# Start addresses of matmul operand tiles moved apart by 32 to 256 bytes, and two weight units multiplied in token halves

## What is computed

```python
# first block
p = rms_norm(x, norm1_g) @ w_in                  # then attention, gated delta, two gated linear mixers
x = x + mixed @ w_out
x = x + conv_glu_ffn(rms_norm(x, norm2_g), w_up, ffn_conv_w, ffn_conv_b, w_down)
# second block
h = h + short_conv_mixer(rms_norm_2(h, g), conv_w_in, conv_w, conv_w_out)
h = h + swiglu_ffn(rms_norm_2(h, g), conv_ffn_w13, conv_ffn_w2)
h = h + mla_mixer(rms_norm_2(h, g), w_dq, ..., w_o, k_nope, k_pe, v, cos, sin)
h = h + swiglu_ffn(rms_norm_2(h, g), mla_ffn_w13, mla_ffn_w2)
return rms_norm_2(h, final_norm_g)
```

## Time and profile before

| what | value |
|---|---|
| time, median of 2 runs | 1940.74 us (1940.49 to 1941.0) |
| span of the profiled execution | 1938.3 us |
| TensorE busy | 1890.5 us, 98% of the span |
| TensorE weight loads busy | 1540.8 us, 79% |
| VectorE, ScalarE, GpSimd busy | 959.2, 739.5, 237.1 us |
| TensorE in the chain that ended last | 91% |
| mean granted TensorE clock | 0.986 of full |
| bytes moved by DMA | 161.34 MB, mean 83 GB/s |

### The profile page before, as it was taken

One profiled execution on the slowest core, in us unless ns is written; L12 is line 12 of the kernel. 1 busy time (PEld: TensorE's weight loads), 2 busy tenths in 40 slices (PEclk: granted clock), 3 DMA queues, 4 the chain that ended last, 5 costly groups with the idle time before them and its releaser, 6 DMA issues.

```text
span 1938.3 us, 25963 instructions
## 1 busy us (share of the span) xinstructions
PE 1890.5 (98%) x9271; PEld 1540.8 (79%) x9271; DVE 959.2 (49%) x1354; ACT 739.5 (38%) x1075; POOL 237.1 (12%) x196
## 2 busy tenths in 40 slices
PE   8989999999999999999999999999999999999998
PEld 6778867667888888888888888888776778888887
DVE  6464466654777763344454444333647444444322
ACT  6542543554444443232253333232455343333222
POOL 0051000102111111000021111101000121111100
PEclk9999998999999999999999999999999999999999
DMA  6310211113333333333333333333320133333332
GB/s 193 87 33 1 55 34 34 34 47 89 103 97 97 94 94 94 98 98 98 98 88 104 94 95 97 92 99 101 92 83 22 44 95 94 94 96 96 100 90 73
DMA packets 309223, 161.34 MB, mean 83 GB/s; under 512 B 12688, under 2 KB 306832, under 8 KB 309024
## 3 DMA queue, kind: packets, MB, share of 16 engines
q1 hardware_dynamic: 308080, 157.67, 28.1%
q0 software_dynamic: 640, 2.17, 0.3%
q10 hardware_dynamic: 432, 0.52, 0.1%
HBM read 158.24 MB, written 2.10 MB: 83 GB/s over the span
## 4 chain that ended last, share of the span: by engine, by line
PE 91%; DVE 4%; ACT 3%; issue 1%; POOL 0%; DMA 0%; ACTq 0%; DVEq 0%; POOLq 0%
PE ps L371 26%; PE ps L372 26%; PE ps L373 26%; PE ps L1063 1%; PE ps L1743 1%; PE ps L1491 1%; PE ps L1075 1%; PE ps L1501 1%; PE ps L2039 1%; PE ps L2040 1%; PE ps L1734 1%; PE ps L936 1%; ACT whi L358 1%; PE ps L920 1%; PE ps L1455 0%
## 5 line engine op out<-in xcount | busy, mean ns | idle before, releaser
L371 PE MATMUL ps<-xhi,whi 128*128 128x512 f32 x1656 | 656.6, 396 | 3.1 <-ACT ecol L989 2.1
L372 PE MATMUL ps<-xlo,whi 128*128 128x512 f32 x1656 | 647.7, 391 | 0.0
L373 PE MATMUL ps<-xhi,wlo 128*128 128x512 f32 x1656 | 647.6, 391 | 0.0
L358 ACT ACTIVATE whi<-raw 128x1024 fp32r<-128x1024 f32 (+2 forms) x297 | 309.0, 1040 | 707.6 <-PE ps L373 707.0
L366 DVE TENSOR_TENSOR wlo<-raw,whi 128x1024 fp32r<-128x1024 f32 (+2 forms) x297 | 365.8, 1232 | 278.6 <-ACT whi L358 278.6
L371 PEld LDWEIGHTS ps<-xhi,whi 128*128 128x128 f32 x1656 | 313.1, 189 | 72.1 <-issue 7.9
L373 PEld LDWEIGHTS ps<-xhi,wlo 128*128 128x128 f32 x1656 | 312.8, 189 | 65.9
L372 PEld LDWEIGHTS ps<-xlo,whi 128*128 128x128 f32 x1656 | 313.1, 189 | 65.3 <-issue 2.2
L621 DVE TENSOR_TENSOR zS<-ps,rs 128x512 f32<-128x512 f32 x132 | 91.3, 692 | 296.8 <-PE ps L373 284.6
L373 PE MATMUL ps<-h_hi,wlo 128*128 128x512 f32 x528 | 205.4, 389 | 0.0
L371 PE MATMUL ps<-h_hi,whi 128*128 128x512 f32 x528 | 205.4, 389 | 0.0
(11 more groups left out here) (339 smaller groups left out, 1718.7 us busy)
## 6 DMA issues: line engine op xcount, KB each, us to landing
raw<-in_conv_ffn_w SPq DMA_DIRECT2D x52, 512.0 KB, 3.8
raw<-in_mla_ffn_w SPq DMA_DIRECT2D x52, 512.0 KB, 3.8
raw<-in_w_up SPq DMA_DIRECT2D x44, 512.0 KB, 3.8
raw<-in_w_in SPq DMA_DIRECT2D x28, 512.0 KB, 3.8
raw<-in_conv_w_in SPq DMA_DIRECT2D x24, 512.0 KB, 3.7
raw<-in_w_down SPq DMA_DIRECT2D x16, 448.0 KB, 3.5
raw<-in_conv_ffn_w SPq DMA_DIRECT2D x16, 448.0 KB, 3.5
raw<-in_mla_ffn_w SPq DMA_DIRECT2D x16, 448.0 KB, 3.4
```

Source lines behind the costliest of these rows:

```text
L358: a.activation(whi[:, u % PARTS, 0:n], raw[:, u % RAW, 0:n], ACT.Copy).then_inc(hi_split, 1)
L371: t_.matmul(out, wh, xh, start=first, stop=False)
L372: t_.matmul(out, wh, xl, start=False, stop=False)
L373: return t_.matmul(out, wl, xh, start=False, stop=last)
```

## The change

Three things are done.

1. Empty tiles (`gap_...`) are put between tiles, and `raw`, `whi` and `wlo` are cut into one tensor per place, so that `whi0`/`wlo0` (even units) and `whi1`/`wlo1` (odd units) start at different addresses modulo 512. Indexing changes from `whi[:, u % PARTS, ...]` to `whi[u % PARTS][:, ...]`. No instruction is added by it.
2. In units 9 and 10 of `w_in` each matmul over 512 tokens becomes two over 256: first all 8 slices of tokens 0 to 255, then all 8 of tokens 256 to 511. The weights of a slice are loaded once for each half. The waits and the semaphore at the end are the same.
3. All tiles behind move with the gaps.

The start of each operand tile modulo 512 bytes, from the sizes in the order of the calls:

| tile | before | after |
|---|---|---|
| `xT`, `xhi` | 128 | 128 |
| `xlo` | 128 | 192 |
| `raw`, `whi` and `wlo` of even units | 128 | 192 |
| `whi` and `wlo` of odd units | 128 | 448 |
| `h_hi` | 128 | 0 |
| `h_lo` | 128 | 64 |
| `c_hi` | 128 | 0 |
| `c_lo` | 128 | 32 |
| `h3_hi` | 128 | 32 |
| `h3_lo` | 128 | 96 |
| `mx`, `kn`, `qn`, `qp`, `vtok`, `lhi`, `chi` | 128 | 0 |
| `cst` (`hsum`, `ones` start 516 and 1028 bytes behind it) | 128 | 448 |
| `sq`, `ssq`, `rs`, `xg` | 160 | 480 |

The distance of a streamed slice from the weight slice that is used with it (streamed start less weight start, modulo 512) was 0 for all products of `passes`. Now it is, for even and odd units: `xhi` 448 and 192, `xlo` 0 and 256, `h_hi` 320 and 64, `h_lo` 384 and 128, `c_hi` 320 and 64, `c_lo` 352 and 96, `h3_hi` 352 and 96, `h3_lo` 416 and 160.

```diff
--- before.py
+++ after.py
@@ -247,10 +247,13 @@
 
         xT = sb("xT", [P, KT, T])
         xhi = sb("xhi", [P, KT, T], F32R)
+        sb("gap_xlo", [P, 16])
         xlo = sb("xlo", [P, KT, T], F32R)
-        raw = sb("raw", [P, RAW, UNIT])
-        whi = sb("whi", [P, PARTS, UNIT], F32R)
-        wlo = sb("wlo", [P, PARTS, UNIT], F32R)
+        raw = [sb(f"raw{n}", [P, UNIT]) for n in range(RAW)]
+        whi0, wlo0 = sb("whi0", [P, UNIT], F32R), sb("wlo0", [P, UNIT], F32R)
+        sb("gap_odd", [P, 64])
+        whi1, wlo1 = sb("whi1", [P, UNIT], F32R), sb("wlo1", [P, UNIT], F32R)
+        whi, wlo = [whi0, whi1], [wlo0, wlo1]
         cst = sb("cst", [P, NCONST])
         pcol = sb("pcol", [P, NPCOL])
         gbias = sb("gbias", [P, 4])
@@ -260,6 +263,7 @@
         xg = sb("xg", [P, 2, T])
         stat = sb("stat", [P, 4, 4])
         credit = sb("credit", [P, 104])
+        sb("gap_h", [P, 16])
         ps = ctx.enter_context(nc.psum_tensor("ps", [P, 8, T], F32))
         NRING = 6
 
@@ -313,7 +317,7 @@
 
         def unit_view(buf, u):
             _, kt, n, _ = UNITS[u]
-            return buf[:, u % (RAW if buf is raw else PARTS), 0:kt * n].rearrange("p (k c) -> p k c", c=n)
+            return buf[u % len(buf)][:, 0:kt * n].rearrange("p (k c) -> p k c", c=n)
 
         def is_past(u, i, per):
             return u + (per * i if isinstance(i, int) else 0) >= len(UNITS)
@@ -355,7 +359,7 @@
             act.wait_ge(unit_loaded[u % RAW], in_loop(LOADED[u], i, 16 * per // RAW))
             if u >= PARTS:
                 act.wait_ge(unit_used, in_loop(u - PARTS + 1, i, per))
-            a.activation(whi[:, u % PARTS, 0:n], raw[:, u % RAW, 0:n], ACT.Copy).then_inc(hi_split, 1)
+            a.activation(whi[u % PARTS][:, 0:n], raw[u % RAW][:, 0:n], ACT.Copy).then_inc(hi_split, 1)
 
         def split_lo(dve, u, i=None, per=0, e=v):
 
@@ -363,7 +367,7 @@
                 return
             n = elements(u, i, per)
             dve.wait_ge(hi_split, in_loop(u + 1, i, per))
-            e.tensor_tensor(wlo[:, u % PARTS, 0:n], raw[:, u % RAW, 0:n], f32(whi[:, u % PARTS, 0:n]),
+            e.tensor_tensor(wlo[u % PARTS][:, 0:n], raw[u % RAW][:, 0:n], f32(whi[u % PARTS][:, 0:n]),
                             ALU.subtract).then_inc(lo_split, 1)
 
         def passes(out, wh, wl, xh, xl, first, last):
@@ -860,6 +864,14 @@
                         pe_load_last(pe)
                 return
             pe.wait_ge(*after(f"in{u - 2} taken" if u >= 2 else f"x{KT - 2} taken"))
+            if u in (9, 10):
+                pe.wait_ge(lo_split, u + 1)
+                for half in (slice(0, T // 2), slice(T // 2, T)):
+                    for k in range(KT):
+                        wh, wl = (unit_view(b, u)[:, k, :] for b in (whi, wlo))
+                        last = passes(acc(u)[:, half], wh, wl, xhi[:, k, half], xlo[:, k, half], k == 0, k == KT - 1)
+                last.then_inc(unit_used, 1)
+                return
             product(pe, u, u, ks=ks)
 
         def act_copy_in(act, u, dst, scale=1.0):
@@ -1906,11 +1918,13 @@
         mixers.close()
         ffn = ctx.enter_context(ExitStack())
         h_hi = sb("h_hi", [P, FT, T], F32R, ffn)
+        sb("gap_h_lo", [P, 16], F32, ffn)
         h_lo = sb("h_lo", [P, FT, T], F32R, ffn)
         zS, yg, yu = (sb(n, [P, 2, T], F32, ffn) for n in ("zS", "yg", "yu"))
         ffn.close()
         conv = ctx.enter_context(ExitStack())
         c_hi = sb("c_hi", [P, KT, T], F32R, conv)
+        sb("gap_c_lo", [P, 8], F32, conv)
         c_lo = sb("c_lo", [P, KT, T], F32R, conv)
         bS, cS, vS, yS = (sb(n, [P, 2, T], F32, conv) for n in ("bS", "cS", "vS", "yS"))
         r2 = sb("r2", [P, T], c=conv)
@@ -1938,7 +1952,9 @@
         attn.close()
         mla.close()
         ffn3 = ctx.enter_context(ExitStack())
+        sb("gap_h3", [P, 8], F32, ffn3)
         h3_hi = sb("h3_hi", [P, FT, T], F32R, ffn3)
+        sb("gap_h3_lo", [P, 16], F32, ffn3)
         h3_lo = sb("h3_lo", [P, FT, T], F32R, ffn3)
         zS3, yg3 = (sb(n, [P, 2, T], F32, ffn3) for n in ("zS3", "yg3"))
         ffn3.close()
```

## The result

The changed kernel takes 1986.96 us (median of 2 runs, 1986.33 to 1987.59), slower by 46 us. The comparison of all runs puts it at 1.0248 times the kernel before (95% interval 1.0208 to 1.0288); the two medians alone give 1.0238. The forecast was 1941.4 us and no change.

The account below looks back on a forecast made before the run. TensorE's float32r matmul pace was taken to bound the kernel: span 1938.3 + 0 + 0 + 0.64 = 1938.9 us, with 2.4 us between span and median 1941.4 us; range 1938 to 1955 us.

Parts of the forecast that it names:

- What bounds the kernel: TensorE, busy 98% of the span; 6948 float32r matmuls at 0.2266 us each make 1574 us, 81% of 1938.3 us.
- New addresses, TensorE: Changed distance between streamed slice and loaded weights, for 6120 matmuls; claimed no effect on the step, 0 us.
- Rows 4, no scatter: Loop stretches with VectorE busy 35.33 and 20.91 us of 50 hold 222 and 223 matmuls; read as no memory contest.
- Rows 5, plain float32 matmuls at other distances: Plain float32 matmuls at distances 28, 252 and 0 all take 592 ns; read, with a caution, as no distance effect.
- Rows 7, the unloaded record: A product's last matmul, no load behind it, has 0.39 us like its neighbour; weak sign the surplus isn't from loads.
- The Trainium skill's rule: TensorE's two read ports, for stream and weight loads, are independent and it never waits; taken as agreeing with no effect.
- Slower rival: Float32r matmuls at unequal starts: stream crosses load and waits 14 ns, 6120 of them, 85.7 us, 2027.1 us; chance 0.07.
- Faster rival: Float32r matmuls: equal start causes the 13.3 ns surplus; other distances save 81.4 us over 6120, giving 1860.0 us; chance 0.08.
- Token halves: Units 9 and 10, 96 matmuls of 256 columns: surplus goes with the instruction, 11.52 us for 10.88, +0.64 us, all counting.
- Starts at odd multiples of 32: Streams of `c_lo`, `h3_hi`, `h3_lo`, 592 matmuls: taken as 0, with 3.9 us kept for the range.
- Range: Kernel time from 1938 to 1955 us, held at 0.85, covering dearer halves and odd starts but neither rival.

Follow-up runs that it names:

- addresses_only: Changed kernel with all its new addresses, but units 9 and 10 in matmuls of 512 columns as before; 1985.85 us, 1.0236 times the kernel before.
- weights_64: Kernel before with all streamed tiles at 128 and all weights at 192, so only the stream-to-weights distance changes; 1985.92 us, 1.0229 times before.
- odd_256: Kernel before with only the weights of odd units 256 bytes further, distances 0 and 256; 1940.53 us, 1.0001 times before.
- load_widths: Kernel before at distance 0, units 3 to 10 with 32, 96 or 64 weight columns or cut into 384 and 128 tokens; 1943.31 us, 1.0019.
- halves_only: Kernel before with its addresses, only units 9 and 10 in halves of 256 columns; 1939.91 us, 0.9997 times before.
- fine_distances: Kernel before with high and low tiles at one start, x 128, h 160, c 96, h3 192, weights at 132 (even units) and 144 (odd); 1973.44 us, 1.0175.
- wlo_16: Kernel before with all streams and high weights at one start modulo 256, low weights 16 bytes before it; 1946.78 us, 1.004 times before.
- interleaved: Kernel before with high and low weights of a unit stored number by number, so loads step 8 bytes; 1990.63 us, 1.0273 times before.

## Why the prediction was wrong

**What bounds the kernel**: right. The step between float32r matmuls, 81% of the span, decided, and nothing else did. (The row of the granted clock has one slice under 9, not two; no number rests on it.)

**New addresses, TensorE, taken as 0**: this step failed. It measured 46 us (`addresses_only`), 6.6 ns for each of 6948 matmuls. Three readings had stood for it, and each was misread:

- Rows 4, no scatter. A pace without scatter was taken as a sign that stream and load don't touch each other; the runs speak for a fixed rhythm of the two instead. After a stall the trace of before has two to nine steps between 224 and 236 ns until it finds 227. These were there to be read: they are steps of float32r matmuls out of rhythm, and their mean, 230.5 to 232.0 a stall, is close to what the changed kernel pays throughout (230 to 237).
- Rows 5, plain float32 matmuls at other distances. They stay at 592 ns at half the rate of float32r; the caution written beside it, that this leaves twice the time for a second reader, fits that, though no run tests it. The changed kernel has `grow`, now at distance 60, at 592 again. (`sq`, still at 28, has a mean of 634 there, but only because three of its 32 records, near 268 us, fell into a stretch at granted clock 0.5; the others keep 592.)
- Rows 7, the unloaded record. Whether its surplus has to do with a load stays open, and the record, whose end is modelled, says nothing of other distances.

**The Trainium skill's rule**, two read ports independent of each other and TensorE never waiting ("SBUF — State Buffer", "Who interferes with whom"), was weighed as agreeing. `weights_64` and `odd_256` disagree with it as far as it would make the weights' address irrelevant: the same streams and loads differ by 6.6 ns a matmul at distance 192 and by nothing at 256. The measurement decides.

**Slower rival**: the right side, and its reason "every product was at distance 0, so a cost at others could not have shown" was the truth of the case; it had a chance of 0.07. Its price of 14 ns was twice the 6.6 measured, and its mechanism, a crossing of stream and load from unequal starts, isn't shown: `load_widths` has longer steps at the equal start too. Its count was wrong too: it left `xlo` against even units out as being at distance 0, and exactly that matmul has the longest step, 237.4 ns, with its neighbours at other distances.

**Faster rival**: the equal start was the good case, not the bad one. No measured distance goes below 226.7.

**Token halves**: right. An instruction's share of the surplus gave 11.52 us, `halves_only` has 11.51, and unit 11 starts at 79.55 where it was 79.06 while unit 9 started 0.14 earlier: the 0.63 us reach the chain in full. The kernel's time, 0.9997 of before, is too coarse to show them. At the addresses of the changed kernel the 96 halves took 11.30 us.

**Starts at odd multiples of 32**: no cost of their own. `h` at 160 in `fine_distances` has 226.7 ns.

**Range**: it went to 1955 and left out the slower rival. With the addresses' effect unseen by any row, it should have taken in both rivals, from 1860 to 2027.

## What to carry to other kernels

Let all tiles that float32r matmuls stream one after another start alike modulo 256 bytes, high and low parts included, and let the weights start there too. Weights 16 or 28 bytes before the streams did as well where high and low weights of a unit stood alike (the down products of `fine_distances`), but low weights alone 16 bytes ahead were not safe (`wlo_16`). If an edit adds a small tile ahead of them, fill it up to a multiple of 256. A pace without any scatter can be a rhythm that an address holds up: look for the steps after a stall, which show the price of losing it. Where every row of a trace has one value of what a change moves, the trace can't give that change a price, and the range has to keep both signs.

## What the hardware showed that was not expected

- The step of back-to-back 128x512 float32r matmuls depends on the start of the streamed slice against the weights and against the stream before, modulo 256 bytes: medians of 226.7 ns at 0, 16 and 28 bytes and of 229.5 to 234.5 at 17 distances outside, some 2.3% of this kernel when all units are outside (`weights_64`). Five units outside had the fast step all the same.
- The fast step is the column time at 2.4 GHz plus 13.3 ns for 256, 384 and 512 columns alike (120.0, 173.3, 226.7 ns); with 128 columns the step is 109 to 115 ns.
- Loads of 32, 64 or 96 weight columns don't shorten a step; at distance 0 they lengthened it to 231.7, 230.2 and 230.6 ns.
- The rhythm has memory: with low weights 16 bytes ahead of the high ones, the same loop ran at 231 ns a step in one stage and at 226.7 in another of the same execution.
- Halves of 256 columns are faster at the changed kernel's addresses (117.7 ns) than at distance 0 (119.9), the other way round from 512 columns.
- Weights streamed at an 8-byte step take 453 ns for 512 columns, against 227 when they are contiguous (`interleaved`).
